# The last pair of experts: pair 6's down step behind pair 7's up, and TensorE's branch ahead of pair 7's down

## The reference

```python
p_group = jax.nn.softmax(t @ wg_r + bg_r)            # 4 groups, the best one is taken
g_val, g_idx = lax.top_k(p_group, 1)
top_v, top_i = lax.top_k(sel, TOP_K)                 # two experts of the group's four
...
for e in range(N_EXPERTS):                           # 16 experts, D = 1024, hidden 512
    h = jax.nn.silu(t @ w_gate[e]) * (t @ w_up[e])
    out = out + combine[:, e:e + 1] * (h @ w_down[e])
...
return rmsnorm(h, norm_final)[:, N_META:]
```

## Time and profile before

| | us |
|---|---|
| median of 3 runs (1665.22 to 1666.05) | 1665.5 |
| the profiled execution | 1665.6 |
| its span in the trace | 1663.8 |
| TensorE busy | 1590.2 (96%) |
| VectorE busy | 830.3 (50%) |
| ScalarE busy | 735.2 (44%) |

### The profile page before, as it was taken

One profiled execution on the slowest core, in us unless ns is written; L12 is line 12 of the kernel. 1 busy time (PEld: TensorE's weight loads), 2 busy tenths in 40 slices (PEclk: granted clock), 3 DMA queues, 4 the chain that ended last, 5 costly groups with the idle time before them and its releaser, 6 DMA issues.

```text
span 1663.8 us, 26843 instructions
## 1 busy us (share of the span) xinstructions
PE 1590.2 (96%) x11188; PEld 1227.4 (74%) x11188; DVE 830.3 (50%) x1461; ACT 735.2 (44%) x1140; POOL 0.9 (0%) x5
## 2 busy tenths in 40 slices
PE   8999989999999999999889899999999989999987
PEld 5646567777787778689768899998988778535443
DVE  2536664634333344542675766655677764312223
ACT  3444552633213332442463654546545543455443
POOL 0000000000000000000000000000000000000000
PEclk9999999999999999999999999999999999999999
DMA  9412523254334433423202345452442227799995
GB/s 390 150 39 102 203 102 104 99 198 157 135 106 164 190 121 99 173 77 127 101 1 77 129 159 208 166 177 99 167 140 102 77 102 289 318 403 421 421 420 209
DMA packets 43133, 287.89 MB, mean 173 GB/s; under 512 B 4849, under 2 KB 6001, under 8 KB 12161
## 3 DMA queue, kind: packets, MB, share of 16 engines
q1 hardware_dynamic: 42832, 285.99, 45.6%
q10 hardware_dynamic: 144, 0.06, 0.0%
q0 software_dynamic: 32, 0.07, 0.0%
HBM read 285.05 MB, written 1.05 MB: 172 GB/s over the span
## 4 chain that ended last, share of the span: by engine, by line
PE 80%; DVE 9%; ACT 5%; DMA 4%; issue 2%; DVEq 0%; SPq 0%; ACTq 0%
PE ps L539 17%; PE ps L540 16%; PE ps L541 16%; PE ps L2936 7%; DMA deep<-wts 4%; DVE WL L524 2%; PE ps L584 2%; PE ps L2796 1%; PE ps L1553 1%; PE ps L1524 1%; PE ps L1455 1%; PE ps L564 1%; PE ps L702 1%; PE ps L1632 1%; PE ps L1631 1%
## 5 line engine op out<-in xcount | busy, mean ns | idle before, releaser
L539 PE MATMUL ps<-HH,WH 128*128 128x512 f32 (+2 forms) x1488 | 495.5, 333 | 20.8 <-DVE WL L524 11.0
L541 PE MATMUL ps<-HH,WL 128*128 128x512 f32 (+2 forms) x1488 | 483.8, 325 | 0.0
L540 PE MATMUL ps<-HL,WH 128*128 128x512 f32 (+2 forms) x1488 | 483.6, 325 | 0.0
L524 DVE TENSOR_TENSOR WL<-ring,WH 128x2048 fp32r<-128x2048 f32 (+2 forms) x134 | 281.6, 2104 | 146.7 <-ACT WH L514 146.7
L539 PEld LDWEIGHTS ps<-HH,WH 128*128 128x128 f32 x1488 | 284.4, 191 | 70.6 <-issue 31.6
L541 PEld LDWEIGHTS ps<-HH,WL 128*128 128x128 f32 x1488 | 284.3, 191 | 21.8
L514 ACT ACTIVATE WH<-ring 128x2048 fp32r<-128x2048 f32 (+2 forms) x134 | 235.8, 1761 | 144.5 <-DMA ring<-wts 77.1
L540 PEld LDWEIGHTS ps<-HL,WH 128*128 128x128 f32 x1488 | 284.9, 191 | 19.7
L2936 PE MATMUL ps<-deep,arena 128*32 128x512 f32 (+1 forms) x872 | 114.0, 593 | 10.7 <-ACT late_x L2922 5.6
L539 PE MATMUL ps<-parts,WH 128*128 128x512 f32 (+1 forms) x352 | 119.7, 340 | 0.0
L540 PE MATMUL ps<-parts,WH 128*128 128x512 f32 (+1 forms) x352 | 118.4, 336 | 0.0
(11 more groups left out here) (400 smaller groups left out, 2107.3 us busy)
## 6 DMA issues: line engine op xcount, KB each, us to landing
ring<-wts SPq DMA_DIRECT2D x138, 1024.0 KB, 4.9
deep<-wts SPq DMA_DIRECT2D x92, 1024.0 KB, 16.5
ring<-wts SPq DMA_DIRECT2D x32, 704.0 KB, 4.0
arena<-wts SPq DMA_DIRECT2D x8, 1024.0 KB, 15.4
ring<-wts SPq DMA_DIRECT2D x4, 672.0 KB, 13.7
X<-xin SPq DMA_DIRECT2D x4, 512.0 KB, 16.4
ahead<-wts SPq DMA_DIRECT2D x2, 1024.0 KB, 8.7
deep<-wts SPq DMA_DIRECT2D x4, 512.0 KB, 20.6
```

The source lines that it names most:

```text
L524: e.tensor_tensor(lo, raw(i), hi.bitcast(F32), ALU.subtract).then_inc(*up("low", i))
L539: e.matmul(o, w[0][:, cols], x[0], start=k == 0, stop=False)
L540: e.matmul(o, w[0][:, cols], x[1], start=False, stop=False)
L541: return e.matmul(o, w[1][:, cols], x[0], start=False, stop=k == nk - 1)
```

## The change

1. Chunk order: of the last pair the up steps come ahead of pair 6's down steps, so that the last eight steps are gate 7, up 7, down 6, down 7 (before: gate 7, down 6, up 7, down 7).
2. TensorE follows: up 7; the first half of down 6; pair 7's transposes; the second half of down 6; the scatter of pair 6; the branch; down 7; the scatter of pair 7. The flag's register load goes ahead of up 7, and the branch from behind down 7 to ahead of it.
3. ScalarE: the copies in the new order; the silu stays behind the first copy of up 7; the output tiles of pair 6 are copied behind both copies for down 6 and ahead of those for down 7. Its branch stays behind the copies for down 7.
4. VectorE: the product of pair 7 ahead of the flag's load; the copy to HT2, then the low parts of pair 6's output, then its additions.
5. Inside the body for crowded groups: it waits for pair 6's down rather than pair 7's, may use all 8 banks, and waits until pair 7's h has been copied.

```diff
@@ chunk_plan
         if e < NP:
             p += [(("eg", x, i), 2048) for i in range(2) for x in (e, partner(e))]
+        if e == NP - 1:
+            p += [(("eu", x, i), 2048) for i in range(2) for x in (e, partner(e))]
         if e:
             p += [(("ed", x, i), 2048) for i in range(2) for x in (e - 1, partner(e - 1))]
-        if e < NP:
+        if e < NP - 1:
             p += [(("eu", x, i), 2048) for i in range(2) for x in (e, partner(e))]
@@ pe_experts
                 if p + 2 < NP:
                     pe_turn_slots(e, p + 2)
+                if p == NP - 1:
+                    break
                 if p:
                     pe_pair_out(e, p - 1, 0)
                     pe_pair_out(e, p - 1, 1)
                 pe_pair_in(e, "eu", p)
-                if p + 1 < NP:
-                    pe_side(e, p + 1)
+                pe_side(e, p + 1)
+            flag_load(e, "pe")
+            pe_pair_in(e, "eu", NP - 1)
+            pe_pair_out(e, NP - 2, 0)
             pe_pair_turn(e, NP - 1)
-            flag_load(e, "pe")
+            pe_pair_out(e, NP - 2, 1)
             pe_scatter(e, NP - 2)
+            with over_capacity(e, "pe"):
+                pe_over(e)
             pe_pair_out(e, NP - 1, 0)
             pe_pair_out(e, NP - 1, 1)
-            with over_capacity(e, "pe"):
-                pe_over(e)
             pe_scatter(e, NP - 1)
@@ act_experts
-            for p in range(NP):
+            for p in range(NP - 1):
...
                 act_other(e, "eu", p, 1)
-                if p + 1 < NP:
-                    act_other(e, "eg", p + 1, 0)
-                    act_other(e, "eg", p + 1, 1)
+                act_other(e, "eg", p + 1, 0)
+                act_other(e, "eg", p + 1, 1)
+            act_other(e, "eu", NP - 1, 0)
+            act_silu(e, NP - 1)
+            act_other(e, "eu", NP - 1, 1)
+            act_other(e, "ed", NP - 2, 0)
+            act_other(e, "ed", NP - 2, 1)
             flag_load(e, "act")
+            act_y(e, NP - 2)
             act_other(e, "ed", NP - 1, 0)
             act_other(e, "ed", NP - 1, 1)
@@ dve_experts
+                if p == NP - 1:
+                    break
                 if p:
                     dve_y(e, p - 1)
                 dve_up(e, p)
+            dve_up(e, NP - 1)
             flag_load(e, "dve")
             dve_pair_turn(e, NP - 1)
+            dve_y(e, NP - 2)
             dve_scatter(e, NP - 2)
@@ pe_over
-            over_banks.order = [b for b in range(8) if b not in (banks.of["ey", NP - 1, 0], banks.of["ey", NP - 1, 1])]
+            e.wait_ge(*at("ht", NP - 1))
             e.wait_ge(*at("added", NP - 2, 7))
@@ act_over, dve_over, sp_over
-            e.wait_ge(*at("used.pair", chunk_step("ed", NP - 1, 1)))
+            e.wait_ge(*at("used.pair", chunk_step("ed", NP - 2, 1)))
```

## The result

| | median of the runs, us | lowest to highest | runs |
|---|---|---|---|
| before | 1665.7 | 1663.3 to 1669.1 | 20 |
| changed | 1669.4 | 1667.3 to 1673.9 | 20 |

The ratio is 1.0021, with an interval from 1.0014 to 1.0028: the change costs 3.5 us. The predicted time was 1668.3, in a range of 1665.0 to 1671.8. The range held, and the direction of the sum was right, but it was too small by 0.7 against the ratio (1.1 against the median of these runs), and the time came out just past the 0.2% up to which the likeliest case counted as no difference, and past the end of that case's own range (1669.2).

The account below looks back on a forecast made before the run. Expert weight transfers set the pace until 1638.89 us, then a chain of waits on VectorE and TensorE. The +0.06 stands inside the branch's +3.2; less 0.4 at the end gives +2.8: 1668.3 us, range 1665.0 to 1671.8.

Parts of the forecast that it names:

- the likeliest case: One branch fetch, partly behind another, ahead of pair 7's down: 1668.3 us, own range 1667.6 to 1669.2, chance 0.40.
- The steps' order: Ahead of pair 6's scatter: one chain of 1.5 us replaces another, so the scatter starts 0.06 us later.
- ScalarE's copies of pair 7's down: Behind ScalarE's output copies at the end: they run later but cost nothing, with a margin of 0.7 us.
- The branch is a fetch, and its cover goes: TensorE's taken branch fetches instructions for 3.70 us; before, 2.6 were hidden under queued matmuls, in its new place little is.
- Rival C: TensorE's branch is cheap or hidden in its new place; only the -0.4 us at the end is left: 1665.1, chance 0.08.
- Rival A: The branch ends only after TensorE runs empty, at 1643.6; pair 7's down shifts by +1.3: 1666.4 us, chance 0.12.
- Its size: The branch ahead of pair 7's down delays that down step by 3.2 us, the middle of +2.8 and +3.7.
- The term for the useless fetch: A next-page fetch in flight at the branch may delay the branch's own, raising the shift from +2.8 to +3.7 us.
- Rival B: The branch's fetch waits for the useless one to complete; pair 7's down starts +6.3 us later: 1671.4, chance 0.31.
- The end: Behind pair 7's down: the last additions come earlier and the stall in the sums goes, -0.4 us.
- The length of pair 7's down: TensorE's last down step: given no term; the forecast added no time for a slower clock.
- the sign "slower": The call that the whole kernel is measurably slower, beyond about 0.2% (3.3 us): chance 0.37.

Follow-up runs that it names:

- the reorder alone: The changed kernel with TensorE's branch put back behind pair 7's down, the new order of steps kept on all engines: 1666.3 us, ratio 1.000.
- the long hold: New step order, branch at the end, TensorE held ahead of pair 7's down by a wait for a VectorE copy of 1,792 columns: 1670.5 us, ratio 1.0028.
- the branch alone: The kernel before with only TensorE's branch moved ahead of pair 7's down, chunk and step order as before: 1670.3 us, ratio 1.0026.
- the body of one expert: The changed kernel with the unrun body for crowded groups cut from 16 experts to one on every engine: 1671.6 us, ratio 1.0035.
- the body of one wait: The changed kernel with the unrun bodies for crowded groups cut to one wait per engine, a near branch target: 1666.1 us, ratio 1.000.
- the two holds: New step order, branch at the end, TensorE held ahead of pair 7's down by a VectorE copy: 1,024 columns 1667.4 us, 1,792 columns 1670.5 us.
- the branch that isn't taken: The kernel before with the uncrowded path first, so the branch ahead of the last scatter isn't taken; a jump follows the last matmul: 1667.1 us, ratio 1.0002.

## Why the prediction was right, and where it was short

- The steps' order (+0.06 at the scatter's start, nothing else): right. The scatter starts 0.05 later, and the reorder alone has a ratio of 1.000. ScalarE's copies of pair 7's down cost nothing either: e12's first half starts at once behind the scatter.
- The branch is a fetch, and its cover goes: right, and the far against the near target (3.3 to 4.0, once 5.0, against 0.38 us) shows that it is the fetch. Rival C (cheap) falls with the far one. Rival A (TensorE must run empty) falls with the near one, which ended at 1644.9 while the scatter ran until 1646.1; by A it had to last that long.
- Its size: predicted 3.70 plus part of another fetch. TensorE met it 0.68 behind the scatter's start and not 0.91 behind (1641.35 less 1640.44), it took 3.84, and pair 7's down starts 2.65 later, counted from the step's end, where I took +3.2. That is below my lower value of +2.8. The term for the useless fetch (+0.45 on average) was there in one of three traces of the changed kernel (+1.2 on the branch). Rival B, two fetches in series, was seen in none.
- The end: -0.4 predicted, -0.27 measured, inside the bounds of -0.2 and -0.6. The additions follow the last subtract as predicted, 1.30 behind the end of pair 7's down (1656.74 less 1655.44), and no gap is left ahead of the scatter or in the sums.
- The length of pair 7's down: this is the step that failed. I took its 64 matmuls over from before at 7.07 without a word on the clock; they took 8.77, 8.42 and 8.46. It is the whole error of the sum and more: 3.2 - 0.4 = +2.8 predicted, 2.65 + 1.7 - 0.27 = +4.1 in the trace and 3.0 to 3.8 by the ratios of the change and its two repeats.

The rows of before could have told it. I had looked for the clock only behind 1618 us, where it is 1.00. Two stretches much further ahead in the same trace of before, in the same columns:

```profile
294.00:296.00 2.00, 0.00 (x0) 0.00 (x0) 1.91 (x4) 1.97 (x5) 0.00 (x0) 1.00 0.79 270
296.00:298.00 2.00, 1.62 (x5) 1.36 (x6) 2.00 (x5) 1.97 (x4) 0.00 (x0) 0.72 1.00 401
298.00:300.00 2.00, 2.00 (x6) 1.54 (x6) 2.00 (x5) 1.94 (x5) 0.00 (x0) 0.50 0.94 397
...
940.00:942.00 2.00, 0.00 (x0) 0.00 (x0) 1.30 (x3) 1.51 (x4) 0.00 (x0) 1.00 0.00 0
942.00:944.00 2.00, 0.19 (x1) 0.20 (x2) 1.88 (x2) 1.83 (x2) 0.00 (x0) 0.50 0.00 0
944.00:946.00 2.00, 2.00 (x10) 2.00 (x11) 1.25 (x3) 0.61 (x2) 0.00 (x0) 0.50 0.59 123
```

After every window of two us of this trace in which TensorE did nothing (five between 200 and 1664 us: at 294, 694, 824, 940 and 1356), the clock is at half within the next. The gaps that hold those windows are 2.75 to 4.87 us long. The two of 2.75, near 293 and 693 us, stand in all 14 traces, with 3 us of steady matmuls ahead of them, and the slow stretch follows in all 28 cases; a gap of 1.88 near 863 stands in all 14 too, and it follows in 4. My own forecast had TensorE stand from 1642.6 to 1645.35, 2.7 us. With 1.7 for that, it would have been 4.5 and the sign "slower". The range held it all the same, because rival B, which no trace shows, had stretched it: as far as the clock goes, that is luck. The sum came as near as it did because the branch's shift, taken 0.55 too long, made up for a part of the 1.7.

## What to carry to other kernels

A taken branch around a long body is an instruction fetch, 3.3 to 4.0 us here; put it where that much work is queued on the same engine, and don't move it to where the queue is nearly empty. When an edit makes TensorE stand for two or three us, look through the whole trace for such gaps and read the granted clock behind them: some 1.7 us more may go there than the gap itself. And count an edit from the last event that it can't touch: the traces here differ by up to 5.8 us before they come to the place.

## What the runs showed that I had not expected

- The slow clock depends on chance as well as on the gap. Six traces have pair 7's down held back with nothing queued ahead of it, by 4.3 us or more behind the scatter's start. Four have the slow stretch in it (the changed kernel's three with 4.79, 4.92 and 6.12, and the long hold with 4.45). Two don't: the branch alone with 4.71, and the body of one expert with 4.34. By TensorE's idle time just ahead of it the four are 2.53, 2.66, 3.86 and 2.19, the two 2.46 and 2.07, so neither length parts them. The branch alone is the only one of the six without the idle 1.5 us ahead of the scatter; no run tells whether it is that or chance. The Trainium skill (TensorE: Matmul & The Clock Gate, What's actually happening) says that the same kernel catches more or fewer slow matmuls from run to run; the traces agree.
- The executions of one kernel differ with the clock too: those of the changed kernel's first repeat took 1667.1 to 1669.3 at clock 0.988 (5 runs) and 1670.5 to 1673.9 at 0.986 and 0.987 (6 runs). The traces have such differences far ahead of the change. Behind the same gap of 1.88, the same stretch of before and then of the changed kernel (columns as in the earlier trace rows):

```profile
864.00:870.00 6.00, 3.47 (x21) 3.09 (x22) 2.86 (x7) 3.36 (x9) 0.00 (x0) 1.00 0.00 0
864.00:870.00 6.00, 4.90 (x20) 4.24 (x20) 2.14 (x5) 1.81 (x4) 0.00 (x0) 0.72 0.00 0
```

- Added up between 200 us and pair 7's down, leaving out its own slow stretch, the time at half clock takes three values. It is 30.7 us in three traces (before and the two holds), whose step's end is at 1636.5 to 1638.9; 34.1 in nine, the changed kernel's first and third among them, at 1639.1 to 1640.5; and 37.6 in two (the body of one wait, and the changed kernel's first repeat), at 1642.0 and 1642.3. So the 1.45 us by which the changed kernel's trace came late to the step's end go with one slow stretch more. The change isn't what brings it: the two kernels made from the one before (the branch alone, and the branch that isn't taken) have 34.1 too.
- A fetch at the end of the program may cost something though no engine waits for it: the three outputs landed 0.4 to 1.7 us later in the two kernels that had it there. The cause wasn't isolated.
- A page end behind a branch's target can stall again: 1.13 us in pair 7's down of the kernel with one expert in the body, 0.70 in the sums of before.
